# Forgetting attention: the causal mask is added to the diagonal score blocks in PSUM by VectorE and no longer multiplied in by TensorE

## The chip, the core and the metric

One core of one Trainium2 chip runs the whole program. The metric is the device time of one execution in microseconds (us). The engines are named as in the profile: PE is TensorE (PEld its weight loads), DVE is VectorE, ACT is ScalarE, POOL is GpSimd, SP is SyncE, which here only issues DMAs.

## What is computed

One layer of a decoder with two attention branches over a prompt of 2048 positions, and a small sampled batch beside it. The change touches one branch for the prompt, the forgetting attention with 8 heads of 64:

```python
def _forgetting_attn(q, k, v, F_q, F_k, q_pos, k_pos):
    s = jnp.einsum('bqhd,bkhd->bhqk', q, k, preferred_element_type=jnp.float32) * (DH_B ** -0.5)
    s = s + jnp.swapaxes(F_q, 1, 2)[..., :, None] - jnp.swapaxes(F_k, 1, 2)[..., None, :]
    s = jnp.where(q_pos[:, None] >= k_pos[None, :], s, NEG_INF)
    p = jax.nn.softmax(s, axis=-1)
    return jnp.einsum('bhqk,bkhd->bqhd', p.astype(v.dtype), v)
```

Keys and forget sums enter as extra rows of the products, and a bound on each query's maximum has been found in an earlier stage, so that the exponential can be taken of a score as it leaves TensorE.

## The kernel before

The program is a row of stages: projections, gates and maxima, differential attention (`attention_a`), forgetting attention (`attention_b`, line 2045), the sampled batch, and the merge. Each stage has one written-out instruction stream for each engine, and engines meet only at semaphores (`wait_ge`, `then_inc`). The diff touches `attention_b` alone.

`attention_b` works in **steps** `(u, g, kt)` (line 2052): head `u` of 8, group `g` of four tiles of queries (512 queries), and a pair of key tiles `kt`, `kt + 1` of 128 keys. Scores lie transposed, keys on partitions and queries along the free dimension. A group begins with its two diagonal steps, `kt = 4g` and `kt = 4g + 2`, and goes on with the full steps before the diagonal. A full step has two blocks of 512 queries, 1024 columns. A diagonal step leaves out queries that come before the keys (`tile_width`, line 2056): the first has 512 + 384 = 896 columns, the second 256 + 128 = 384. The head's groups have 2, 4, 6 and 8 steps, so a head has 20 steps, 8 of them diagonal, and the stage has N = 160 steps, 64 of them diagonal. I write D1 and D2 for the two diagonal steps and F for a full one: a head is D1 D2, D1 D2 F F, D1 D2 F F F F, D1 D2 F F F F F F.

What each engine does for step n:

- **TensorE**, `scores(n)` (line 2162): for each of the two key tiles two products of the same shape, `k2`×`q2` (line 2178) and `km`×`qm` (line 2179), into place n % 3 of `s_ps`. In a diagonal step a 128x128 product of `ident_b` with `mask_q` (line 2184) adds 0 or -1e30 to the triangle of each block: both of them at the end of a D1, one behind each block of a D2. The last product tells `s_done`.
- **ScalarE** (line 2122): waits for `s_done`, writes the exponential of the scores from PSUM to `pf`, tells `p_done`. Behind the exponential of the step after a group's last one it runs `take` (line 2111), which waits for that last step's value products and copies the group's sums out of PSUM.
- **VectorE**: `cast(n)` (line 2134) rounds `pf` to `p_hi` and tells `hi_done`, `low(n)` (line 2139) writes the rest to `p_lo` and tells `split_done`. `finish` (lines 2146 and 2150) divides a group's sums, two steps after its last one.
- **TensorE**, the value products of step n (lines 2217 to 2219): for each key tile `v_hi`×`p_hi`, `v_hi`×`p_lo`, `v_lo`×`p_hi`, behind a wait for `split_done`.

The order on TensorE is written out with AHEAD = 2: `scores(n + 2)`, then perhaps `turn` (four transposes of a finished group, line 2194), then the wait for `low(n)` and the value products of step n. The order on VectorE is `cast(n)`, `low(n)`, perhaps `finish`. `mask_q` is a constant 128x128 tile in bf16, made by GpSimd in the first stage (line 287); a product with it stands in the differential attention as well (line 1996), which the change leaves as it is.

Of the kernel before, what the change touches and what calls it, by code (L numbers as in the profile page):

```python
# [24 lines left out]
P = 128  # L25
# [4 lines left out]
ALU = mybir.AluOpType  # L30
# [2014 lines left out]
def attention_b(k):  # L2045


    nc, a = k.nc, k.att
# [3 lines left out]
    steps = [(u, g, kt) for u in range(HB) for g in range(NGR) for kt in (4 * g, 4 * g + 2, *range(0, 4 * g, 2))]  # L2052
    N, NS = len(steps), len(steps) // HB
    AHEAD, PLACES, PR, HR, LATE, OR = 2, 3, 4, 4, 1, 8
    AUG = DH + 4
    tile_width = lambda g, kt: 512 - P * max(0, kt - 4 * g)
    width = lambda n: sum(tile_width(steps[n][1], steps[n][2] + j) for j in range(2))
    ends = [n for n in range(N) if n + 1 == N or steps[n + 1][1] != steps[n][1]]
    group_of = lambda n: steps[n][0] * NGR + steps[n][1]
    with ExitStack() as ctx:  # L2060
        sb, ps, sem = tools(k, ctx, "att_b")
# [6 lines left out]
        s_ps = ps("s_ps", [P, PLACES, 1024])  # L2068
# [2 lines left out]
            sem(n) for n in ("ones_made", "ones_done", "s_done", "p_done", "hi_done", "split_done", "pv_done"))  # L2071
        acc_read, turned_done, recip_done, o_done = (sem(n) for n in ("acc_read", "turned_done", "recip_done", "o_done"))
        stored = [sem(f"stored{i}") for i in range(OR)]

        with nc.Block() as block:
            @block.sync
# [27 lines left out]
            @block.scalar  # L2104
            def _(act):
                def take(m):
                    G = group_of(m)
                    act.wait_ge(pv_done, m + 1)
                    if G >= 2:
                        act.wait_ge(turned_done, G - 1)  # L2110
                    nc.scalar.activation(o_t[:, G % 2, :], acc[:, G % 2, :], ACT.Copy).then_inc(acc_read, 1)

                act.wait_ge(ones_made, 1)
                for n in range(N):
                    if n % NS == 0 and steps[n][0] < 2:
                        s = steps[n][0]
                        nc.scalar.activation(a.v_hi[s][:, :, dv:P], ones[:], ACT.Copy).then_inc(ones_done, 1)
                    w = width(n)
                    act.wait_ge(s_done, n + 1)
                    if n >= PR:  # L2120
                        act.wait_ge(split_done, n - PR + 1)
                    nc.scalar.activation(pf[:, n % PR, 0:w], s_ps[:, n % PLACES, 0:w], ACT.Exp).then_inc(p_done, 1)  # L2122
                    if n - LATE in ends:
                        take(n - LATE)
                take(N - 1)

            @block.vector
            def _(dve):
                def cast(n):
                    w = width(n)  # L2130
                    dve.wait_ge(p_done, n + 1)
                    if n >= HR:
                        dve.wait_ge(pv_done, n - HR + 1)
                    nc.vector.tensor_copy(p_hi[:, n % HR, 0:w], pf[:, n % PR, 0:w]).then_inc(hi_done, 1)  # L2134

                def low(n):
                    w = width(n)
                    dve.wait_ge(hi_done, n + 1)
                    nc.vector.tensor_tensor(p_lo[:, n % HR, 0:w], pf[:, n % PR, 0:w], p_hi[:, n % HR, 0:w].bitcast(F32),  # L2139
                                            ALU.subtract).then_inc(split_done, 1)  # L2140

                def finish(m):
                    G = group_of(m)
                    view = acc[:, G % 2, :].rearrange("p (j c) -> p j c", j=GROUP)
                    dve.wait_ge(turned_done, G + 1)
                    nc.vector.reciprocal(recip[:, G % 2, :], view[:, :, dv]).then_inc(recip_done, 1)
                    dve.wait_ge(recip_done, G + 1)
                    if G >= OR:
                        dve.wait_ge(stored[G % OR], 16 * (G // OR))
                    nc.vector.tensor_tensor(o[:, G % OR, :, :], view[:, :, 0:dv],  # L2150
                                            recip[:, G % 2, :].unsqueeze(2).to_broadcast([P, GROUP, dv]), ALU.mult).then_inc(o_done, 1)

                for n in range(N):
                    cast(n)
                    low(n)
                    if n - LATE - 1 in ends:
                        finish(n - LATE - 1)
                finish(N - 1)

            @block.tensor  # L2160
            def _(pe):
                def scores(n):
                    u, g, kt = steps[n]
                    s = u % 2
                    both2, bothm = a.b_places[s]
                    q2, k2, qm, km = both2[:, 0, :], both2[:, 1, :], bothm[0:AUG, 0, :], bothm[0:AUG, 1, :]
                    if n % NS == 0:
                        pe.wait_ge(a.b_in[s], 144 * (u // 2 + 1))
                        if u == 1:
                            pe.wait_ge(a.ones_in[1], 48)  # L2170
                    if n >= PLACES:
                        pe.wait_ge(p_done, n - PLACES + 1)
                    at, starts = 0, []
                    for j in range(2):
                        w = tile_width(g, kt + j)
                        qs, ks = slice((g + 1) * 512 - w, (g + 1) * 512), slice((kt + j) * P, (kt + j + 1) * P)
                        out = s_ps[:, n % PLACES, at:at + w]
                        nc.tensor.matmul(out, k2[:, ks], q2[:, qs], start=True, stop=False, skip_group_check=True)
                        last = nc.tensor.matmul(out, km[:, ks], qm[:, qs], start=False, stop=kt < 4 * g, skip_group_check=True)  # L2179
                        if kt >= 4 * g:  # L2180
                            starts.append(at)
                        if j == 1 or kt == 4 * g + 2:
                            for x in starts:
                                last = nc.tensor.matmul(s_ps[:, n % PLACES, x:x + P], k.ident_b[:], k.mask_q[:], start=False, stop=True,
                                                        skip_group_check=True)
                            starts = []
                        at += w
                    last.then_inc(s_done, 1)

                def turn(m):  # L2190
                    G = group_of(m)
                    pe.wait_ge(acc_read, G + 1)
                    for j in range(GROUP):
                        last = nc.tensor.transpose(acc[:, G % 2, j * P:(j + 1) * P], o_t[:, G % 2, j * P:(j + 1) * P], k.ident[:])
                    last.then_inc(turned_done, 1)

                for n in range(AHEAD):
                    scores(n)
                for n, (u, g, kt) in enumerate(steps):
                    if n + AHEAD < N:  # L2200
                        scores(n + AHEAD)
                    if n - LATE in ends:
                        turn(n - LATE)
                    s, G = u % 2, group_of(n)
                    if n % NS == 0:
                        pe.wait_ge(a.b_v_in[s], 32 * (u // 2 + 1))
                        if u < 2:
                            pe.wait_ge(ones_done, u + 1)
                    pe.wait_ge(split_done, n + 1)
                    if kt == 4 * g and G >= 2:  # L2210
                        pe.wait_ge(o_done, G - 1)
                    at = 0
                    for j in range(2):
                        w = tile_width(g, kt + j)
                        hi, lo = p_hi[:, n % HR, at:at + w], p_lo[:, n % HR, at:at + w]
                        out = acc[:, G % 2, 512 - w:512]
                        nc.tensor.matmul(out, a.v_hi[s][:, kt + j, :], hi, start=kt + j == 4 * g, stop=False, skip_group_check=True)
                        nc.tensor.matmul(out, a.v_hi[s][:, kt + j, :], lo, start=False, stop=False, skip_group_check=True)
                        last = nc.tensor.matmul(acc[0:dv, G % 2, 512 - w:512], a.v_lo[s][:, kt + j, 0:dv], hi, start=False, stop=False,
                                                skip_group_check=True)  # L2220
                        at += w
                    last.then_inc(pv_done, 1)
                turn(N - 1)
# [858 lines left out]
```

## Time and profile before

| | us |
|---|---|
| median of 3 runs | 2585.44 |
| lowest and highest | 2583.37, 2587.14 |
| the profiled execution, whole | 2583.07 |
| its span, first to last instruction | 2581.5 |
| busy in the span: PE, DVE, ACT, POOL | 2485.7, 1585.0, 901.4, 187.9 |
| mean granted TensorE clock, as a share | 0.985 |

Busy time of PE is modelled: a product of 512 columns shows 0.40 us, although the next one begins 0.23 us after it, since products overlap in the array. So spacing of starts, not busy time, tells what a product costs. Columns of a timeline are: start (us from the span's start), length (us), engine, line, operation, tensors, shapes, how many are merged into the row, and in brackets the idle time before and what ended it. The forgetting attention runs from about 1692.8 to 2049 us.

### The profile page before, as it was taken

The numbers are of one execution on the slowest core, as the hardware profiler recorded it, in microseconds if no ns is written. First come the engines' busy times: TensorE is split into PE (matmuls) and PEld (weight loads), VectorE is DVE, ScalarE is ACT, GpSimd is POOL, SyncE is SP. The second block draws the span as 40 slices with busy tenths as digits, with TensorE's granted clock in tenths as the row PEclk, the third lists the DMA queues.
The fourth block names the chain that finished last, engine by engine and source line by source line (L and its number), as shares of the span: only waits on it lengthen the run. The fifth ranks groups of instructions, "written<-read, shape, count | busy, mean of one in ns | idle before, by whom it ended". The sixth has DMA issues, their size and how long they took to land. (4 is left out here: it accounts for less than half of the span.)

```text
span 2581.5 us, 34447 instructions
## 1 busy us (share of the span) xinstructions
PE 2485.7 (96%) x12851; PEld 1981.3 (77%) x12851; DVE 1585.0 (61%) x2603; ACT 901.4 (35%) x1433; POOL 187.9 (7%) x182
## 2 busy tenths in 40 slices
PE   5899999999999999999999999999999887999998
PEld 2688888887788878888888778878787654788886
DVE  3321236653666517778887689978878656555554
ACT  4011112224332227785001566644444333222121
POOL 0000112210133100000000300000000000000000
PEclk9999999999999999999999899999999999999999
DMA  8454455545454468665445866447366297543341
GB/s 300 166 214 173 160 172 175 156 154 207 151 165 133 142 222 220 179 159 144 142 136 143 184 148 148 95 81 143 81 133 155 82 328 269 171 130 130 130 129 56
DMA packets 286709, 413.12 MB, mean 160 GB/s; under 512 B 77995, under 2 KB 170507, under 8 KB 277004
## 3 DMA queue, kind: packets, MB, share of 16 engines
q1 hardware_dynamic: 274378, 377.91, 51.2%
q10 hardware_dynamic: 11132, 33.17, 3.5%
q8 instruction: 89, 1.46, 0.2%
q0 software_dynamic: 1056, 0.13, 0.1%
q14 instruction: 54, 0.44, 0.1%
HBM read 273.62 MB, written 137.52 MB: 159 GB/s over the span
## 5 line engine op out<-in xcount | busy, mean ns | idle before, releaser
L1741 DVE CUSTOM_DVE_ANT_0 max_s_ps<-max_s_ps,max_causal 128x128 f32<-128x128 f32 (+7 forms) x256 | 194.3, 769 | 68.9 <-PE max_s_ps L1799 49.6
L708 PE MATMUL proj_z<-first_km,h_hi 128*128 128x512 f32 x576 | 229.6, 399 | 0.0
L708 PE MATMUL proj_z<-first_km,h_lo 128*128 128x512 f32 x576 | 226.0, 392 | 0.0
L708 PE MATMUL proj_z<-first_v,h_hi 128*128 128x512 f32 x576 | 224.6, 390 | 0.0
L2122 ACT ACTIVATE att_b_pf<-att_b_s_ps 128x1024 f32<-128x1024 f32 (+2 forms) x160 | 142.5, 898 | 112.3 <-PE att_b_s_ps L2179 88.2
L1700 ACT ACTIVATE max_s_ps<-max_s_ps,max_neg_top 128x128 f32<-128x128 f32 (+2 forms) x192 | 161.2, 840 | 43.2 <-DVE max_neg_top L1741 31.5
L2139 DVE TENSOR_TENSOR att_b_p_lo<-att_b_pf,att_b_p_hi 128x1024 fp32r<-128x1024 f32 (+2 forms) x160 | 170.5, 1066 | 5.5
L1744 DVE TENSOR_REDUCE max_neg_top<-max_s_ps 128x1 f32<-128x1024 f32 x128 | 154.2, 1225 | 17.9 <-PE max_s_ps L1799 11.4
L708 PE MATMUL proj_z<-proj_w_hi,h_hi 128*128 128x512 f32 x384 | 151.7, 395 | 0.0
L708 PE MATMUL proj_z<-proj_w_hi,h_lo 128*128 128x512 f32 x384 | 149.8, 390 | 0.0
L708 PE MATMUL proj_z<-proj_w_lo,h_hi 128*128 128x512 f32 x384 | 149.5, 389 | 0.0
L2134 DVE CAST att_b_p_hi<-att_b_pf 128x1024 fp32r<-128x1024 f32 (+2 forms) x160 | 97.7, 610 | 67.2 <-ACT att_b_pf L2122 65.8
L1178 ACT ACTIVATE proj_z_sb<-proj_z 128x512 f32<-128x512 f32 x64 | 38.3, 598 | 288.1 <-PE proj_z L708 288.1
L1015 POOL TENSOR_TENSOR proj_rstd<-proj_rstd,keep_neg_half 128x8 f32<-128x8 f32 (+1 forms) x68 | 111.7, 1643 | 322.9 <-DVE proj_rstd L1275 322.9
L708 PEld LDWEIGHTS proj_z<-first_km,h_lo 128*128 128x128 f32 x576 | 108.2, 188 | 24.5
L708 PEld LDWEIGHTS proj_z<-first_v,h_hi 128*128 128x128 f32 x576 | 108.3, 188 | 22.7
L708 PEld LDWEIGHTS proj_z<-first_km,h_hi 128*128 128x128 f32 x576 | 108.3, 188 | 22.3 <-issue 0.8
L1273 DVE TENSOR_REDUCE proj_ss<-proj_sq 128x8 f32<-128x512 f32 (+1 forms) x68 | 46.6, 686 | 123.1 <-ACT proj_sq L1179 123.1
L1798 PE MATMUL max_s_ps<-map_k,map_q 128*128 128x512 f32 (+2 forms) x320 | 115.6, 361 | 0.0
L1943 DVE SCALAR_TENSOR_TENSOR att_a_pc<-att_a_pf,keep_neg_lam 128x1024 f32<-128x1024 f32 (+1 forms) x80 | 89.5, 1119 | 34.5 <-ACT att_a_pf L1923 34.5
L708 PE MATMUL mrg_ps_y<-wo_hi,mrg_uT_hi 128*128 128x512 f32 x256 | 102.7, 401 | 1.6 <-DVE mrg_uT_lo L2438 1.6
L1692 ACT ACTIVATE max_out<-max_z 128x512 f32<-128x512 f32 x48 | 28.6, 596 | 216.1 <-PE max_z L1822 207.7
(438 smaller groups left out, 6127.8 us busy)
## 6 DMA issues: line engine op xcount, KB each, us to landing
w_raw<-in_w_in SPq DMA_DIRECT2D x144, 256.0 KB, 3.8
smp_v_a<-scratch_mixes SPq DMA_DIRECT2D x16, 1024.0 KB, 4.8
map_qm<-scratch_q_hi SPq DMA_DIRECT2D x48, 256.0 KB
map_k<-scratch_k_hi SPq DMA_DIRECT2D x37, 256.0 KB
head_w<-in_w_ada SPq DMA_DIRECT2D x8, 1024.0 KB, 6.2
scratch_mixes<-proj_out SPq DMA_DIRECT2D x32, 256.0 KB, 2.6
scratch_k_hi<-proj_v_hi SPq DMA_DIRECT2D x32, 256.0 KB, 2.4
scratch_k_lo<-proj_v_lo SPq DMA_DIRECT2D x32, 256.0 KB, 2.9
```

The costliest lines, as they stand in the source:

```text
L708: ins = nc.tensor.matmul(out, left(*lt), right(*rt), start=first and n == 0, stop=last and n == len(terms) - 1)
L1015: nc.gpsimd.tensor_tensor(rstd[0:pn, :], rstd[0:pn, :], k.neg_half[0:pn, :], ALU.pow).then_inc(rstd_done, 1)
L1178: nc.scalar.activation(z_sb[0:pn, n % 2, :], src, ACT.Copy)
L1273: step.inc(nc.vector.reduce_sum(ss[0:pn, :], si.rearrange("p (u d) -> p u d", d=DH), AX.X))
L1700: nc.scalar.activation(s, s, ACT.Exp, bias=neg_top[:, kh, u, qt:qt + 1], scale=-1.0 if kh == qh else 1.0, accum_out=sums[:, kh, u, qt:qt + ...
L1741: nc.vector.tensor_tensor_reduce(s, s, causal[:, 1024 - w:1024], -1.0, -NEG, ALU.add, ALU.min, accum_out=neg_top[:, kh, u, qt:qt + 1]).the ...
L1744: nc.vector.tensor_reduce(neg_top[:, kh, u, qt:qt + 1], scores(x), AX.X, ALU.max, negate=True).then_inc(max_done, 1)
L1798: nc.tensor.matmul(o, q2, k2, start=True, stop=False)
L1943: nc.vector.scalar_tensor_tensor(pc[:, m % CR, 0:w], pf[:, m % PR, 1, 0:w], k.neg_lam[:], pf[:, m % PR, 0, 0:w], ALU.mult, ALU.add).then_i ...
L2122: nc.scalar.activation(pf[:, n % PR, 0:w], s_ps[:, n % PLACES, 0:w], ACT.Exp).then_inc(p_done, 1)
L2134: nc.vector.tensor_copy(p_hi[:, n % HR, 0:w], pf[:, n % PR, 0:w]).then_inc(hi_done, 1)
L2139: nc.vector.tensor_tensor(p_lo[:, n % HR, 0:w], pf[:, n % PR, 0:w], p_hi[:, n % HR, 0:w].bitcast(F32), ALU.subtract).then_inc(split_done, 1)
```

## The change

The products with `mask_q` go. VectorE gets a new instruction for each diagonal step, `mask(n)`, which waits for `s_done`, adds `mask_q` in PSUM to the first 128 columns of both blocks (256 columns in one instruction), and tells a new semaphore `masked`. ScalarE's exponential of a diagonal step waits for `masked` in place of `s_done`. In VectorE's stream `mask(n + 2)` stands between `cast(n)` and `low(n)`; the masks of steps 0 and 1 stand ahead of everything.

```diff
+    diagonal = [n for n in range(N) if steps[n][2] >= 4 * steps[n][1]]
+    masked_upto = lambda n: sum(x <= n for x in diagonal)
...
@@ scalar
-                    act.wait_ge(s_done, n + 1)
+                    if n in diagonal:
+                        act.wait_ge(masked, masked_upto(n))
+                    else:
+                        act.wait_ge(s_done, n + 1)
...
@@ vector
+                def mask(n):
+                    u, g, kt = steps[n]
+                    w0 = tile_width(g, kt)
+                    dve.wait_ge(s_done, n + 1)
+                    blocks = s_ps[:, n % PLACES, 0:2 * w0].rearrange("p (j c) -> p j c", j=2)[:, :, 0:P]
+                    nc.vector.tensor_tensor(blocks, blocks, k.mask_q[:].unsqueeze(1).to_broadcast([P, 2, P]), ALU.add).then_inc(masked, 1)
...
+                for n in range(AHEAD):
+                    if n in diagonal:
+                        mask(n)
                 for n in range(N):
                     cast(n)
+                    if n + AHEAD in diagonal:
+                        mask(n + AHEAD)
                     low(n)
...
@@ tensor
-                        last = nc.tensor.matmul(out, km[:, ks], qm[:, qs], start=False, stop=kt < 4 * g, skip_group_check=True)
-                        if kt >= 4 * g:
-                            starts.append(at)
-                        if j == 1 or kt == 4 * g + 2:
-                            for x in starts:
-                                last = nc.tensor.matmul(s_ps[:, n % PLACES, x:x + P], k.ident_b[:], k.mask_q[:], start=False, stop=True,
-                                                        skip_group_check=True)
-                            starts = []
+                        last = nc.tensor.matmul(out, km[:, ks], qm[:, qs], start=False, stop=True, skip_group_check=True)
```

## Rows read from the trace of the kernel before

**Rows 1.** Busy time by stretch: us, then busy us of PE, PEld, DVE, ACT, POOL, clock, DMA share, GB/s
```profile
1692.00:2049.00 357.00, 353.65 (x1856) 280.77 (x1856) 280.08 (x384) 160.40 (x194) 0.95 (x1) 0.99 0.51 108
```

**Rows 2.** PE's timeline around a D1 and D2 that follow full steps
```profile
1806.67 0.39 PE L2178 MATMUL att_b_s_ps<-map_k 128*128 128x512 f32 x1
...
1807.31 0.34 PE L2179 MATMUL att_b_s_ps<-first_km 68*128 68x384 f32 x1
1807.49 0.29 PE L2184 MATMUL att_b_s_ps<-keep_mask_q,keep_ident_b 128*128 128x128 bf16 x2
1807.58 0.48 PE L2217 MATMUL att_b_acc<-att_b_p_hi,first_v 128*128 128x512 f32 x1
...
1809.07 0.28 PE L2178 MATMUL att_b_s_ps<-map_k 128*128 128x256 f32 x1
...
1809.35 0.31 PE L2178 MATMUL att_b_s_ps<-map_k 128*128 128x128 f32 x1
1809.49 0.28 PE L2179 MATMUL att_b_s_ps<-first_km 68*128 68x128 f32 x1
...
1811.12 0.39 PE L2178 MATMUL att_b_s_ps<-map_k 128*128 128x512 f32 x1
```

**Rows 3.** DVE's timeline in the same stretch, one row
```profile
1805.21 1.22 DVE L2139 TENSOR_TENSOR att_b_p_lo<-att_b_pf,att_b_p_hi 128x1024 fp32r<-128x1024 f32 x1
```

**Rows 4.** ACT's timeline in the same stretch, one row
```profile
1807.81 0.92 ACT L2122 ACTIVATE att_b_pf<-att_b_s_ps 128x896 f32<-128x896 f32 x1 [1.31 <-PE att_b_s_ps L2184]
```

**Rows 5.** DVE's groups by shape: line, operation, shapes, count, busy us, mean ns, idle before
```profile
L2150 DVE TENSOR_TENSOR att_b_o<-att_b_acc,att_b_recip 128x256 f32<-128x256 f32 x32 | 13.6, 424 | 1.1
L1741 DVE CUSTOM_DVE_ANT_0 max_s_ps<-max_s_ps,max_causal 128x256 f32<-128x256 f32 x32 | 14.2, 442 | 1.1 <-PE max_s_ps L1799 0.2
L2139 DVE TENSOR_TENSOR att_b_p_lo<-att_b_pf,att_b_p_hi 128x1024 fp32r<-128x1024 f32 x96 | 117.7, 1226 | 3.3
L2139 DVE TENSOR_TENSOR att_b_p_lo<-att_b_pf,att_b_p_hi 128x896 fp32r<-128x896 f32 x32 | 35.0, 1092 | 1.1
L2139 DVE TENSOR_TENSOR att_b_p_lo<-att_b_pf,att_b_p_hi 128x384 fp32r<-128x384 f32 x32 | 17.9, 558 | 1.1
```

**Rows 6.** Timeline of all engines at the stage's last step, where PE waits for DVE
```profile
2043.98 1.23 DVE L2139 TENSOR_TENSOR att_b_p_lo<-att_b_pf,att_b_p_hi 128x1024 fp32r<-128x1024 f32 x1
...
2045.27 0.50 PE L2217 MATMUL att_b_acc<-att_b_p_hi,head_v_hi 128*128 128x512 f32 x1 [0.35 <-DVE att_b_p_lo L2139]
...
2046.52 0.40 PE L2219 MATMUL att_b_acc<-att_b_p_hi,head_v_lo 128*64 128x512 f32 x1
```

**Rows 7.** PE's timeline around a D1 and D2 that follow a D1 and D2
```profile
1829.11 0.40 PE L2178 MATMUL att_b_s_ps<-map_q 128*128 128x512 f32 x1
...
1830.41 0.48 PE L2217 MATMUL att_b_acc<-att_b_p_hi,head_v_hi 128*128 128x512 f32 x1
...
1832.95 0.45 PE L2178 MATMUL att_b_s_ps<-map_q 128*128 128x512 f32 x1
...
1834.30 0.47 PE L2217 MATMUL att_b_acc<-att_b_p_hi,head_v_hi 128*128 128x512 f32 x1
```

**Rows 8.** DVE's timeline in the stretch of rows 7
```profile
1831.19 0.17 DVE L2146 RECIPROCAL att_b_recip<-att_b_acc 128x4 f32<-128x4 f32 x1
...
1832.39 1.09 DVE L2139 TENSOR_TENSOR att_b_p_lo<-att_b_pf,att_b_p_hi 128x896 fp32r<-128x896 f32 x1
```

**Rows 9.** Stretches around the stage's start: us, PE busy, clock, DMA share, GB/s
```profile
1684.00:1688.00 4.00, 2.37 (x9) 1.00 0.22 65
1688.00:1692.00 4.00, 2.50 (x12) 1.00 0.00 0
1692.00:1694.00 2.00, 1.24 (x8) 1.00 0.45 131
1694.00:1698.00 4.00, 3.19 (x13) 0.53 1.04 238
1698.00:1702.00 4.00, 4.00 (x20) 0.62 1.04 221
```

More of the change, by code:

```diff
@@ L2073, in attention_b @@
         stored = [sem(f"stored{i}") for i in range(OR)]
+        masked = sem("masked")
         with nc.Block() as block:
@@ L2172, in scores @@
                         pe.wait_ge(p_done, n - PLACES + 1)
-                    at, starts = 0, []
+                    at = 0
                     for j in range(2):
```

## Prediction

> **What bounds the kernel now.** I read three views, in this order. The busy time by stretch first: over the forgetting attention PE is busy 353.65 of 357 us, while DVE is busy 280 and ACT 160 [rows 1]. So PE sets this stage's pace, and a microsecond that PE stands idle there is a microsecond of the whole. The timelines of PE and DVE next, because what matters is not DVE's share but *when* its work is done. DVE finishes `low` of the last-but-one full step before a D1 at 1805.21 + 1.22 = 1806.43; PE asks for it only at 1807.58, behind `scores(D1)` [rows 2, 3]. So each `low(n)` is done some 1.15 us before PE needs it, and this lead is why PE never waits. It comes from order: `low(n)` hangs only on the exponential of step n, which was ready long before `scores(n + 2)` began. The groups by shape give the durations [rows 5].
>
> **What is removed.** 128 mask products, four in each of 32 groups. Measured by starts: from the start of `scores(D1)` to the start of `scores(D2)` is 1809.07 - 1806.67 = 2.40 us. The score products take 1807.49 - 1806.67 = 0.82, a 384 wide product 1807.49 - 1807.31 = 0.18, so a 512 wide one (0.82 - 0.36) / 2 = 0.23, and six value products 1.40. So the masks, with the stumble of the weight load behind them, cost 0.18. In D2 the same is 1811.12 - 1809.07 = 2.05 against 0.12 + 0.12 for the 256 wide products (half of a 512 wide one), 0.10 for the first 128 wide one (a quarter would be 0.06; today 1809.49 - 1809.35 = 0.14 with a mask's load in between; I take the middle), 0.06 for the second, and 1.40 + 0.06 for the value products, whose first weight load a short product hides less. That is 1.86: the masks cost 0.19 [rows 2]. Together 0.37 x 32 = 12 us, all of it on the engine that sets the pace. If nothing else happened, this would be the gain.
>
> **What is added on DVE.** 64 instructions of 256 columns that read and write PSUM. The kernel has no such add with a bf16 operand. Nearest rows: a tensor_tensor of 256 columns out of PSUM at 424 ns, and the maxima stage's mask-and-reduce of 256 columns from PSUM to PSUM at 442 ns [rows 5]. I take 0.44, the row with both ends in PSUM; the other bound is 0.42. A following instruction starts some 0.08 before the end of the one ahead, so it moves `low` by 0.36. As throughput this is 64 x 0.36 = 23 us beside 280 of 357: hidden. As latency it isn't, which is the next part.
>
> **What the new wait does.** `mask(n + 2)` waits for `scores(n + 2)`, and `low(n)` is queued behind it on DVE. PE, having issued `scores(n + 2)`, goes straight on to wait for `low(n)`. So in each diagonal step `low(n)` can no longer be done ahead: it starts only when PE has finished the scores, behind the mask. PE then stands idle for the end of the last product, the mask, and a whole `low`. `cast(n)` is ahead of the mask and stays hidden, and `mask` itself delays ACT's exponential harmlessly (its result is wanted two steps later).
>
> *A pair D1, D2 behind full steps.* Clock at 0 when `scores(D1)` starts. Its last product starts at 0.64 and ends at 0.98; a waiter starts some 0.04 after (today ACT starts at 1807.81, the masks end at 1807.49 + 0.29 = 1807.78) [rows 2, 4]. Mask 1.02; `low` from 1.38 to 2.60 (1.226) [rows 5]. From the end of `low` to PE's first value product is 0.06, and six value products after such a wait take 1.48: `low` ends at 2045.21, PE starts at 2045.27, the sixth starts at 2046.52 and takes 0.23 more [rows 6]. So the step ends at 2.60 + 0.06 + 1.48 = 4.14, against 2.40: +1.74. D2: the last of its score products starts at 0.12 + 0.12 + 0.10 = 0.34 and ends at 0.62; mask at 0.66, `low` from 1.02 to 2.24, step done at 3.78 against 2.05: +1.73. The pair costs 3.47, with the saving of the masks already in it.
>
> *A pair behind a D1 and a D2* (the second group of a head, 8 times). The steps whose `low` is late are short: 1.092 and 0.558 us [rows 5]. From the start of `scores(D1)`: mask 1.02, `low` 1.38 to 2.47, value products from 2.53, against 1.30 today (1830.41 - 1829.11). They take 1.29, so `scores(D2)` starts at 3.82; mask 4.48, `low` 4.84 to 5.40, value products 5.46, and they take 0.67: 6.13, against 3.84 today (1832.95 - 1829.11): +2.29 [rows 7]. Then DVE, free at 5.32, has `finish` and a cast to do (1832.39 - 1831.19 = 1.20 until `low` starts) and a `low` of 1.09, and is done at 7.61, PE ready 0.06 later; with scores and `turn` (1834.30 - 1832.95 = 1.35) PE is there at 7.48 [rows 7, 8]: +0.19 more. Together 2.48.
>
> *Behind a pair* the next masks are at least two steps away, over the stage DVE has 280 us of work for PE's 354 [rows 1], so DVE has its lead back and nothing more is lost. Nothing is won back either, since PE is the pace.
>
> **The sum.** A head has three pairs of the first kind and one of the second: 3 x 3.47 + 2.48 = 12.89. Eight heads: 103.1. The first pair of the first head has no step ahead of it to delay: -3.5. So +99.6. On the profiled execution 2583.07 + 99.6 = 2682.7; the median lies 2.4 above that execution, so 2685. Each of 62 delayed steps may be off by 0.15 us (the end of a product is modelled; mask 0.42 or 0.44): 9 us either way. DMAs are not moved; stores of finished groups come later with their groups and are far from any wait.
>
> **Rivals.**
>
> *The clock falls too.* At the stage's start PE was busy 2.37, 2.50 and 1.24 us in stretches of 4, 4 and 2 us, and then the granted clock went from 1.00 to 0.53 (that is 1.2 GHz for nearly all of the stretch, where 2.4 is the upper level) and 0.62 [rows 9]. Lost: 4 x 0.47 + 4 x 0.38 = 3.4 us of PE. In a late pair PE would be idle about 1.7 us, busy 1.9, idle 1.7 (an end shows 0.16 to 0.22 after the next start is due): about as thinly as before that fall, though the full clock held through the first two of those stretches. If it falls at all 31 pairs: 31 x 3.4 = 105 more, 2790; if only in the longer double pairs of each head, 8 x 3.4 = 27 more, 2712. A middle of half the pairs: 53 more, 2738. For it: the fall at 1694. Against: 8 us of equally thin work before it without one, and full work after each pair. The Trainium skill ("TensorE: Matmul & The Clock Gate", Part 1) says that a block watches how busy PE is, halves its clock when it has been idle and grants the full clock after sustained work; its warning on oscillation is about repeated waits for DMA, longer than these. By that reading of the page the fall would not come from these waits.
>
> *The lead holds (faster).* If `low(n)` were not held up, for instance if DVE could run it while the mask waits, or the scores were done a whole mask and `low` (0.36 + 1.22 us) before PE reaches its wait, only the 12 us of products would count: 2573. It decides at the point where `scores(n + 2)` ends 1.6 us or more before the value products of step n are due. In PE's order the two touch [rows 2], so I see no room. The Trainium skill ("PSUM — Partial Sum Buffer", Engine vs sequencer instructions) has VectorE's queue as strictly first in, first out, which also excludes overtaking; the rows of DVE show no instruction out of its written order.
>
> *The delay spreads.* If after each group DVE's lag makes one more step late by about 0.5 us (a late exponential behind `take`, then a late cast), 32 x 0.5 = 16 more: 2701. The slack that I find in a first kind pair is near 1 us at the next step (by the same steps `low(D1)` is done 0.1 us after D2's value products end, 1.2 before PE asks for it behind a full `scores` and `turn`), which speaks against it.
>
> **How the numbers follow.** The forecast has 0.62, the clock 0.25, the spread delay 0.08, the lead 0.03, and 0.02 that some cover I missed cancels the loss nearly exactly. Range: down from 2685 by 9 for the terms and as much again for a mask wait somewhat better covered, 2665; up over the spread delay and the middle of the clock case, 2765. The measurement tells 0.2%, about 5 us, from no change: faster 0.03, same 0.01, slower 0.96.
>
> **What would show it.** In the profile after: PE idle before line 2217 some 62 times, 1.0 to 1.7 us each, put down to DVE's `p_lo`, about 95 us in all; the mask near 0.44; PE's busy share of the stage near 0.76; the stage about 457 us long; the DVE idle before the mask, ended by PE's scores. Wrong would be: idle of PE under 1 us at these places, a clock below 0.98 within the stage (then the rival), or a `low(n)` that starts before its mask.

## The result, and the profile after

| | us |
|---|---|
| before, median of 4 runs | 2586.29 (2583.37 to 2589.46) |
| changed, median of 4 runs | 2712.12 (2699.46 to 2715.47) |
| ratio | 1.0487, 95% interval 1.0468 to 1.0506 |
| the profiled execution, whole, and its span | 2709.66, 2708.1 |

The kernel is 125.8 us slower. The forecast was 2685, about 100 slower, in a range of 2665 to 2765. So the direction, the place and most of the size came as forecast, and some 26 us came on top.

The page of the changed kernel, its first lines: PE has 33 us *more* busy time than before, though 128 products fewer.

```profile
span 2708.1 us, 34255 instructions
## 1 busy us (share of the span) xinstructions
PE 2519.1 (93%) x12723; PEld 2001.1 (74%) x12723; DVE 1601.5 (59%) x2667; ACT 900.8 (33%) x1433; POOL 189.0 (7%) x182
```

Busy time by stretch over the forgetting attention of the changed kernel (us, busy of PE, PEld, DVE, ACT, POOL, clock, DMA share, GB/s), to be held against [rows 1], and below it the kernel before over the like stretch. Both stretches begin at 1705, behind the fall of the clock at the stage's start that [rows 9] shows, so they leave out the stage's first 12 us:

```profile
1705.00:2175.00 470.00, 380.92 (x1686) 292.44 (x1684) 289.60 (x433) 155.15 (x187) 0.00 (x0) 0.91 0.36 76
```

```profile
1705.00:2049.00 344.00, 342.23 (x1804) 271.51 (x1802) 273.86 (x373) 155.23 (x187) 0.00 (x0) 1.00 0.50 104
```

Two things differ from before. PE is no longer busy all the time (381 of 470, where it was 342 of 344), and the granted clock is 0.91 where it was 1.00. The first is the forecast's loss, the second its main rival.

Who waited for whom in the stage (engine, line, what, us in total, times, the longest). DVE's new instruction waits 141 us for PE's scores, and PE, of which the weight load (PEld) waits first, waits for DVE's `low`. Between 1702 and 2044 us of the kernel before PE waits for nothing:

```profile
DVE att_b_s_ps L2147 <- PE att_b_s_ps L2197: 140.6, 62, 3.2
PEld att_b_acc L2228 <- DVE att_b_p_lo L2152: 98.0, 62, 2.0
PE att_b_acc L2228 <- DVE att_b_p_lo L2152: 87.5, 57, 2.6
```

62 times is the number of delayed steps that the prediction counted; the row of PE shows 57, one of them the wait at the stage's last step that [rows 6] has too, and for 6 more at the same place, of 1.05 us at most, the profile names no releaser. One pair of diagonal steps behind full steps, on PE, answering to [rows 2]. The first line is the start of `scores(D1)`, then the two value products that waited, and the start of the next full step's scores:

```profile
1767.68 0.45 PE L2196 MATMUL att_b_s_ps<-map_q 128*128 128x512 f32 x1
...
1770.37 0.49 PE L2228 MATMUL att_b_acc<-att_b_p_hi,head_v_hi 128*128 128x512 f32 x1 [1.65 <-DVE att_b_p_lo L2152]
...
1774.08 0.50 PE L2228 MATMUL att_b_acc<-att_b_p_hi,head_v_hi 128*128 128x512 f32 x1 [1.65 <-DVE att_b_p_lo L2152]
...
1775.58 0.39 PE L2196 MATMUL att_b_s_ps<-map_q 128*128 128x512 f32 x1
```

The pair takes 1775.58 - 1767.68 = 7.90 us where it took 4.45 [rows 2]: +3.45. The clock stayed at 1.00 throughout this pair, so this is the price of the delay alone. DVE's side of another such pair, answering to [rows 3], shows the order that does it: the mask stands idle until the scores are done, and the `low` whose data were ready long before comes after it:

```profile
1749.10 0.43 DVE L2147 TENSOR_TENSOR att_b_s_ps<-att_b_s_ps,keep_mask_q 128x256 f32<-128x256 f32 x1 [2.80 <-PE att_b_s_ps L2197]
1749.44 1.22 DVE L2152 TENSOR_TENSOR att_b_p_lo<-att_b_pf,att_b_p_hi 128x1024 fp32r<-128x1024 f32 x1
```

The new instruction by shape, answering to [rows 5] (mean 432 ns, between the two bounds of 424 and 442):

```profile
L2147 DVE TENSOR_TENSOR att_b_s_ps<-att_b_s_ps,keep_mask_q 128x256 f32<-128x256 f32 x64 | 27.6, 432 | 140.6 <-PE att_b_s_ps L2197 140.6
```

### The profile page after: what moved, and what is told of

It reads as the page before. It is cut to its first block and busy times, and to the rows that moved or that the text cites. A ratio compares the mean times of both kernels' runs of the same rounds, so it can differ in the third digit from the quotient of the medians.

```text
span 2708.1 us, 34255 instructions
## 1 busy us (share of the span) xinstructions
PE 2519.1 (93%) x12723; PEld 2001.1 (74%) x12723; DVE 1601.5 (59%) x2667; ACT 900.8 (33%) x1433; POOL 189.0 (7%) x182
## 5 line engine op out<-in xcount | busy, mean ns | idle before, releaser
L1744 DVE TENSOR_REDUCE max_neg_top<-max_s_ps 128x1 f32<-128x1024 f32 x128 | 154.2, 1224 | 17.9 <-PE max_s_ps L1799 11.5
L2228 PE MATMUL att_b_acc<-att_b_p_hi,first_v 128*128 128x512 f32 (+3 forms) x160 | 67.3, 421 | 48.6 <-DVE att_b_p_lo L2152 46.1
L2147 DVE TENSOR_TENSOR att_b_s_ps<-att_b_s_ps,keep_mask_q 128x256 f32<-128x256 f32 x64 | 27.6, 432 | 140.6 <-PE att_b_s_ps L2197 140.6
```

Of the source, the lines that this page charges most:

```text
L1744: nc.vector.tensor_reduce(neg_top[:, kh, u, qt:qt + 1], scores(x), AX.X, ALU.max, negate=True).then_inc(max_done, 1)
```

## The experiments

Two questions were open: whether it is the wait's place in VectorE's queue that costs, or the mask instruction; and what the 26 us are. Each kernel was timed beside the kernel before on its own chip, whose median was 2581.65, 2586.51 and 2583.29 us in the three groups. I give differences to that.

### What was removed, alone

`e_gone` is the changed kernel without VectorE's masks: the products are gone and nothing is in their place, so it leaves out the causal mask of this branch.

```diff
-                    if n in diagonal:
-                        act.wait_ge(masked, masked_upto(n))
-                    else:
-                        act.wait_ge(s_done, n + 1)
+                    act.wait_ge(s_done, n + 1)
...
-                    nc.scalar.activation(pf[:, n % PR, 0:w], s_ps[:, n % PLACES, 0:w], ACT.Exp).then_inc(p_done, 1)
+                    nc.scalar.activation(pf[:, n % PR, 0:w], s_ps[:, n % PLACES, 0:w], ACT.Exp,
+                                         scale=0.001 if n in diagonal else 1.0).then_inc(p_done, 1)
...
-                    if n + AHEAD in diagonal:
-                        mask(n + AHEAD)
```

> No mask at all: the 128 products with mask_q are gone and nothing takes their place (the causal mask on the diagonal blocks of the forgetting attention is left out, and ScalarE takes the exponential of a thousandth of the score there, so that it stays finite). This measures the part that was removed, by itself. If my prices of the products are right (0.18 us in a D1, 0.19 in a D2, 32 of each), the time is 12 us under before, near 2574. If the products had been hidden, it is within 4 us of before.

Measured: 2573.52, ratio 0.9967 (0.9955 to 0.998), so 8.1 us gained by the medians, 5 to 12 by the interval. The products were on the path, and 12 us was at the upper end of what they cost. The trace shows where it fell short: a pair behind full steps takes 4.08 us where it took 4.47 (medians of 23 pairs; -0.39, forecast -0.37), but a pair behind a D1 and a D2 only 3.63 where it took 3.84 (medians of 7; -0.21).

### The wait without the mask instruction

`e_wait` is the kernel before, with this in VectorE's stream:

```diff
                     cast(n)
+                    if n + AHEAD < N and steps[n + AHEAD][2] >= 4 * steps[n + AHEAD][1]:
+                        dve.wait_ge(s_done, n + AHEAD + 1)
                     low(n)
```

> The kernel before, with its mask products on TensorE, and one wait added: between cast(n) and low(n) VectorE waits until scores(n + 2) are done, if n + 2 is a diagonal step. No mask instruction on VectorE. Theory one (the place of the wait is the cause): low(n) starts only after the scores, PE idles for the rest of a product and a whole low; by the steps of the prediction +3.0 us in a pair behind full steps and +2.0 in one behind a D1 and a D2, 3 x 3.0 + 2.0 = 11.1 in a head, 89 less the first pair = +86 at full clock, 2672, and with clock falls as in the changed kernel some 20 to 25 more, 2690 to 2700. Rival (the mask instruction itself, on PSUM or with its bf16 operand, is what costs): within 10 us of before, since no such instruction is there.

Measured: 2669.66, ratio 1.0338 (1.0315 to 1.0361), +88.0. The rival falls: a wait alone, with no instruction on VectorE added and all products still on TensorE, makes the loss. The sum at full clock was +86, and it came out. The 20 to 25 us that I had added for the clock did not come: from 1705 on it stayed at 1.00, as the stretch shows (columns as above), while PE's waits, in the second fence, came to 68 us, with 1.3 us as the longest.

```profile
1705.00:2135.00 430.00, 358.80 (x1816) 277.24 (x1814) 271.17 (x377) 156.47 (x189) 0.00 (x0) 1.00 0.40 84
```

```profile
PE att_b_acc L2219 <- DVE att_b_p_lo L2139: 68.4, 57, 1.3
```

### PE's idle time filled with products nobody reads

`e_fill` is the changed kernel, with work for PE where it waits:

```diff
+                def fill(n):
+                    both2 = a.b_places[steps[n][0] % 2][0]
+                    pe.wait_ge(p_done, n + 1)
+                    for i in range(4 if n in diagonal else 7):
+                        nc.tensor.matmul(s_ps[:, n % PLACES, 0:512], both2[:, 1, 0:P], both2[:, 0, 0:512], start=True, stop=True,
+                                         skip_group_check=True)
...
+                    if n + AHEAD in diagonal:
+                        fill(n)
                     pe.wait_ge(split_done, n + 1)
```

> The changed kernel, with idle time of PE filled: ahead of the wait for low(n) in a step that is delayed PE issues 7 products of 512 columns (4 where n itself is a diagonal step) into the place of s_ps that the exponential of step n has left and that scores(n + 3) will overwrite; their result is never read. 7 x 0.23 = 1.64 us fit into the 1.84 us that PE would stand still. If the 26 us above my 99.6 are the clock's, which falls because PE is idle, then this kernel with more work on PE is faster than the changed one: mean clock near 0.985, near 2686 (+100), no wait of DVE shorter. If they come from something else, the time stays near 2712 or above it.

Measured: 2677.57 (2677.24 to 2677.73), ratio 1.0368 (1.0346 to 1.039), +95.9. PE has 386 products more to do (46 x 7 + 16 x 4), and still the loss is 95.9 us and not 125.8. The clock is full over the stretch:

```profile
1705.00:2142.00 437.00, 435.16 (x2057) 331.80 (x2055) 288.36 (x431) 155.05 (x187) 0.00 (x0) 1.00 0.39 82
```

More work on PE, a full clock and a shorter time: the 26 us are the clock's. The remaining loss is the delayed `low`, and it is worth about what the steps of the prediction gave.

`e_fill2` has `range(2)` in place of `range(4 if n in diagonal else 7)`.

> As the kernel with filled idle time, but only 2 products of 512 columns (0.47 us) in each delayed step, so that PE still shows about 1.2 us idle there. The kernel with the wait alone had idle times near 1.3 us and no fall of the clock in the stage. If the fall depends on how thin the work is over a pair, this is enough: mean clock near 0.985, 2675 to 2682. If some falls remain, 2685 to 2705.

Measured: 2680.6, ratio 1.0366 (1.0343 to 1.0389), +94.1. Two products of 512 columns in each delayed step are enough for a full clock, and on the same chip the changed kernel without them (`e_same`, below) took 2705.55, so they save 25 us:

```profile
1705.00:2145.00 440.00, 379.39 (x1818) 286.11 (x1817) 292.75 (x440) 156.83 (x189) 0.00 (x0) 1.00 0.40 83
```

This run also shows a pair behind a D1 and a D2 undisturbed by the clock (PE's timeline, starts of `scores(D1)`, of `scores(D2)`, of the next full step's scores, and of the value products after it):

```profile
1756.79 0.40 PE L2196 MATMUL att_b_s_ps<-map_q 128*128 128x512 f32 x1
...
1760.62 0.28 PE L2196 MATMUL att_b_s_ps<-map_q 128*128 128x256 f32 x1
...
1762.86 0.46 PE L2196 MATMUL att_b_s_ps<-map_q 128*128 128x512 f32 x1
...
1764.38 0.50 PE L2237 MATMUL att_b_acc<-att_b_p_hi,head_v_hi 128*128 128x512 f32 x1
```

1762.86 - 1756.79 = 6.07 against 3.84 [rows 7]: +2.23, and 1.52 in place of 1.35 to the next value products: +0.17. A pair behind full steps takes 7.85 us in this run, the median of 23, against 4.47 in the kernel before: +3.38.

### The changed kernel again

`e_same` has no edit.

> The changed kernel once more, beside the others on one chip. It says how much its time varies with the falls of the clock: 2700 to 2715 as before if the falls come at each execution; near 2680 if they depend on the chip.

Measured: 2705.55 (2698.16 to 2718.59), ratio 1.0483 (1.0453 to 1.0513), +119.0. Its four executions order by their mean granted clock: 2698.16 at 0.978, 2702.83 at 0.973, 2708.27 at 0.972, 2718.59 at 0.968. The filled kernel's four executions lie within 0.5 us, this one's within 20. In its profiled execution the stage ran at 0.95 of the clock, in the other profile at 0.91, and the span is 11.5 us shorter. Read in stretches of 0.5 us, this profile has 9 slow stretches from 1710 on, the other 17:

```profile
1710.00:2163.00 453.00, 363.55 (x1688) 279.44 (x1686) 289.49 (x433) 155.28 (x187) 0.00 (x0) 0.95 0.37 78
```

### Half of the change

`e_d2` masks the second diagonal step of a group as the changed kernel does, and the first one with products as before.

```diff
-    diagonal = [n for n in range(N) if steps[n][2] >= 4 * steps[n][1]]
+    diagonal = [n for n in range(N) if steps[n][2] == 4 * steps[n][1] + 2]
...
-                        last = nc.tensor.matmul(out, km[:, ks], qm[:, qs], start=False, stop=True, skip_group_check=True)
+                        last = nc.tensor.matmul(out, km[:, ks], qm[:, qs], start=False, stop=kt != 4 * g, skip_group_check=True)
                         at += w
+                    if kt == 4 * g:
+                        for x in (0, 512):
+                            last = nc.tensor.matmul(s_ps[:, n % PLACES, x:x + P], k.ident_b[:], k.mask_q[:], start=False, stop=True,
+                                                    skip_group_check=True)
                     last.then_inc(s_done, 1)
```

> Half of the change: the second diagonal step of each group is masked by VectorE as in the changed kernel, the first by the products on TensorE as before. Each delayed step costs by itself: +1.73 in three groups of a head and +1.25 in the one behind a D1 and a D2, 6.44 x 8 - 1.7 = +50 at full clock, 2631. PE now has one idle time of 1.65 us with full work around it in place of two within 4 us: if the clock needs both to fall, it holds near 0.985 and the time is 2628 to 2636; if one is enough, mean clock below 0.98 and the time 2640 or more.

Measured: 2661.38, ratio 1.0301 (1.0277 to 1.0325), +74.9, where full clock would have given +50. One idle time in a group is enough for the clock to fall; my idea that it takes two near each other was wrong. From 1705 on the profile has 23 waits of 1.65 us, and behind 18 of them, within 1.5 us of their end, a slow stretch begins; behind the waits of 0.98 us, those of the groups that follow a D1 and a D2, none does. PE's timeline and the stretches around one fall show it:

```profile
1764.45 0.50 PE L2232 MATMUL att_b_acc<-att_b_p_hi,head_v_hi 128*128 128x512 f32 x1 [1.65 <-DVE att_b_p_lo L2152]
...
1765.49 0.56 PE L2233 MATMUL att_b_acc<-att_b_p_lo,head_v_hi 128*128 128x512 f32 x1
1765.84 0.63 PE L2234 MATMUL att_b_acc<-att_b_p_hi,head_v_lo 128*64 128x512 f32 x1
```

```profile
1761.00:1765.00 4.00, 2.35 (x12) 1.00 1.02 211
1765.00:1769.00 4.00, 4.00 (x14) 0.57 1.13 176
1769.00:1773.00 4.00, 4.00 (x23) 1.00 1.11 218
```

PE works on after the wait at full clock for one us, then its products go from 0.40 to 0.63 us each in the middle of full work, and are back in the third stretch. (Columns of the stretches: us, PE busy, clock, DMA share, GB/s; 0.57 is the lower level, 1.2 GHz, for most of the stretch.) The fall is paid by work that has nothing to do with the wait.

`e_d2fill` is `e_d2` with the two unread products.

> The half change (second diagonal step masked by VectorE, first on TensorE) with 2 unread products of 512 columns in each delayed step. The half change came out at +75 against a full-clock sum of +50, with a mean clock of 0.975. If the missing 25 us are the clock's, 2 products bring them back: clock near 0.985, +48 to +52, near 2632 to 2637 beside a kernel before of 2581 to 2586. If my price of a D2 step is wrong instead, it stays near +75.

Measured: 2627.91, ratio 1.0175 (1.016 to 1.0191), +44.6, the stage at full clock:

```profile
1705.00:2095.00 390.00, 359.92 (x1806) 276.58 (x1804) 281.47 (x402) 155.12 (x187) 0.00 (x0) 1.00 0.44 91
```

So the clock cost `e_d2` 30 us (74.9 less 44.6), and my +50 for the delays was 5 too high. The trace shows the two sizes that were off: a group's pair takes 6.13 us against 4.47, +1.66 in place of +1.73, and one behind a D1 and a D2 4.84 against 3.84, +1.00 in place of +1.25.

### Other places for the mask

`e_behind` puts it behind `low(n)`.

```diff
                     cast(n)
-                    if n + AHEAD in diagonal:
-                        mask(n + AHEAD)
                     low(n)
+                    if n + AHEAD in diagonal:
+                        mask(n + AHEAD)
```

> The changed kernel with cast(n), low(n), mask(n + 2) in this order: low(n) is no longer behind the mask, but cast(n + 1) and low(n + 1) are. Theory one (a low is late by what is queued ahead of it): low(n) keeps its lead. On the clock of a pair behind full steps the mask of D1 starts at 1.02, cast and low of the next step follow and end at 3.32, PE asks at 2.62: PE stalls about 0.76 once in a pair in place of twice 1.85, pair +0.4 against before. Behind a D1 and a D2 about +0.7. 3 x 0.4 + 0.7 = 1.9 in a head, +15: 2595 to 2602. If any wait for the scores of two steps ahead costs a full low each time, near 2670.

Measured: 2597.92, ratio 1.0051 (1.0034 to 1.0068), +11.4; expected was 2595 to 2602. One short wait in each group is left in place of two long ones, of 0.56 to 0.66 us but for the stage's first (1.5). The row also holds the wait at the stage's last step, which [rows 6] has too:

```profile
PE att_b_acc L2228 <- DVE att_b_p_lo L2152: 19.7, 32, 1.5
```

`e_next` keeps the mask between `cast` and `low` but takes it one step later, when its scores have long been issued:

```diff
-                for n in range(AHEAD):
-                    if n in diagonal:
-                        mask(n)
+                mask(0)
                 for n in range(N):
                     cast(n)
-                    if n + AHEAD in diagonal:
-                        mask(n + AHEAD)
+                    if n + 1 in diagonal:
+                        mask(n + 1)
                     low(n)
```

> The changed kernel with the mask one step later in VectorE's stream: between cast(n) and low(n) stands mask(n + 1) in place of mask(n + 2). scores(n + 1) was issued ahead of the value products of step n - 1, so they are done before low(n) is due. Theory one: low(n) then ends at about 2.60 on the clock of a pair that starts with scores(D1), PE asks for it at 2.62, so nothing or 0.1 us is lost there, the products' 12 us are mostly gained: 2574 to 2580. If the loss came from VectorE's added work or from the longer path of the exponential, it stays well above before, 2600 or more.

Measured: 2575.45, ratio 0.9973 (0.9958 to 0.9987). Timed again as `e_next_again`:

> The kernel with mask(n + 1) between cast(n) and low(n), unchanged, timed again to narrow its interval: 0.996 to 0.998 of before. If the first comparison was luck, the interval includes 1.

2574.4, ratio 0.9969 (0.9956 to 0.9981). Both intervals leave out 1: it is 0.3% faster than before, and within 2 us of the kernel with no mask at all. The same 64 instructions on VectorE, taken one step later, cost nothing that can be measured. The timelines of DVE and PE over a pair:

```profile
1807.21 0.43 DVE L2147 TENSOR_TENSOR att_b_s_ps<-att_b_s_ps,keep_mask_q 128x256 f32<-128x256 f32 x1 [0.46 <-PE att_b_s_ps L2195]
1807.55 1.22 DVE L2152 TENSOR_TENSOR att_b_p_lo<-att_b_pf,att_b_p_hi 128x1024 fp32r<-128x1024 f32 x1
```

```profile
1806.20 0.39 PE L2194 MATMUL att_b_s_ps<-map_k 128*128 128x512 f32 x1
...
1808.82 0.53 PE L2226 MATMUL att_b_acc<-att_b_p_hi,first_v 128*128 128x512 f32 x1
...
1810.36 0.39 PE L2194 MATMUL att_b_s_ps<-map_k 128*128 128x512 f32 x1
```

`low` ends at 1808.77 and PE takes its first product at 1808.82, just as it is due: there is no margin left, but no wait either. The pair takes 4.16 us against 4.45.

## Why the prediction was right, step by step

- **What bounds the stage: right.** PE sets the pace. PE's idle time came back in the time: in `e_behind` PE waits 19.7 us for DVE, the missing products save 8.1 (`e_gone`), and the time is 11.4 longer.
- **The products removed, 12 us: somewhat high.** By starts over one pair I had 0.37 us and took it for all 32 groups; `e_gone` gives 8 us (5 to 12). The pairs behind full steps do give 0.39, those behind a D1 and a D2 only 0.21: 24 x 0.39 + 8 x 0.21 = 11.
- **The mask at 0.44: right** (0.432). That it costs nothing as throughput is shown by `e_next`, in which it runs the same 64 times for free.
- **The delayed `low`: right.** A pair behind full steps +3.38 by the medians, +3.45 by the one shown (forecast 3.47), a pair behind a D1 and a D2 +2.40 (forecast 2.48). Eight heads by the measured pairs: 8 x (3 x 3.38 + 2.40) - 3.38 = 97. `e_fill` with the clock held has +95.9, `e_fill2` +94.1; what is left lies within their 95% intervals, some 6 us either way. That PE's wait would show 62 times and about 95 us in all was right as well (98.0 by the weight loads). Its length was forecast as 1.0 to 1.7 us; it is 1.65 in the pairs behind full steps, 0.7 to 1.05 in the others, and 2.6 once, at the stage's start.
- **Nothing more lost behind a pair: right.** The idle times are those in the pairs, and the delay did not spread. From 1692 to 2175 the stage is 483 us long with PE busy for 0.81 of it, where 457 and 0.76 were forecast; the clock's 26 us, in which PE was mostly busy, are in both.
- **The clock: this is the term that was mis-sized.** I gave the rival 0.25, and the forecast proper had nothing for it. A clock below 0.98 within the stage was named as a sign of being wrong, and it came. It fell behind part of the pairs: 0.91 of the clock over 470 us is 2 x 0.09 x 470 = 85 us at the lower level, and the time came out 26 us above the forecast. Read in stretches of 0.5 us, the lower level comes to 82 us, and PE was busy for 74 of them, so the waits cover little of it. A product of 512 columns begins 0.43 us behind the one before where it was 0.23, by which the slow time costs some 34 us, an estimate; why the medians show less is open. The step that failed was the argument against it, that the clock had held over the 8 us ahead of the stage. That was no evidence of safety: in `e_d2` a fall followed 18 of 23 single idle times of 1.65 us, with full work on both sides, and not the other 5. I also took support from the Trainium skill ("TensorE: Matmul & The Clock Gate", Part 1), reading its warning as one about longer waits than these; the traces here show falls from waits of 1.65 us, so the measurement decides against my reading. On that page the Trainium skill has a second case of oscillation ("A second HAM failure mode"), short idle times between groups of products, which is nearer to this kernel, and I had passed it over. That the rival's case of one double pair in each head gave 2712, the very time that was measured, is luck: it stood for 8 falls of 3.4 us, and the profile shows 17 slow stretches, behind first, third and fourth groups of the heads.
- **The size that I set for one fall (3.4 us): too high.** I had read it from the fall at the stage's start. Most slow stretches behind 1705 are half as long as that one: in `e_d2` 18 of them cost 30 us, 1.7 each.

## What to carry to other kernels

An instruction that waits is a gate for all that is queued behind it on its engine, so ask of a new wait not what it costs its own engine but what ready work stands behind it and who needs that. Here the same instruction between the same two neighbours cost 119 to 126 us when it waited for the newest scores, and the kernel was 6 to 9 us faster than before when it waited for those of one step earlier. And an idle time on TensorE can have a second price beside its length, if the clock falls behind it, as it did here; fill it with unread products to tell the two apart.

## What the runs showed of the hardware that I had not expected

- The clock can fall behind a single idle time on TensorE of 1.65 us, and the 0.40 us products then take 0.63 in full work that follows (`e_d2`). With idle times of 1.32 us, twice in each pair behind full steps, the stage ran at 1.00 from 1705 on (`e_wait`), and so it did with 1.18 us (`e_fill2`). Whether the length of the idle time decides, or what stands around it, no run here tells.
- The falls don't come at the same places in each execution: the changed kernel spreads over 20 us on one chip, by its mean clock; with idle times filled it spreads over 0.5 us (`e_fill`) and 3.6 us (`e_fill2`).
- A kernel can be made faster by work that nobody reads: 2677.57 with 386 unread products, 2705.55 and 2712.12 without; against the kernel before on the same chip +95.9, +119.0 and +125.8.
